# Query projections and expert slots of a PEER layer in one sequence, with the selection of experts in four pieces

## The reference

```python
q = (xc @ w_query).reshape(C, PEER_HEADS, 2, PEER_HALF)          # 8 heads, 2 halves of 128
sc = jnp.einsum('thpd,hpnd->thpn', q, sub_keys)                  # 128 sub-keys a half
top_s, top_i = lax.top_k(sc, 16)
cand_s = (top_s[:, :, 0, :, None] + top_s[:, :, 1, None, :]).reshape(C, PEER_HEADS, 256)
best_s, best_pos = lax.top_k(cand_s, 16)
experts = jnp.take_along_axis(cand_i, best_pos, axis=-1)         # of 16384 experts
gates = jax.nn.softmax(best_s, axis=-1)
u, vv = expert_down[experts], expert_up[experts]
act = jax.nn.gelu(jnp.einsum('cd,chkd->chk', xc, u))
y = jnp.einsum('chk,chkd->cd', gates * act, vv)
```

## Time and profile before

| | us |
|---|---|
| median of three runs (1506.03 to 1508.57) | 1506.32 |
| profiled execution | 1510.51 |
| its span | 1508.7 |
| PE busy | 1271.6 |
| POOL busy | 900.9 |
| DVE busy | 799.8 |
| ACT busy | 598.0 |
| first and last gather issued | 268.1, 918.0 |
| first and last dot starts | 307.9, 939.7 |

### The profile page before, as it was taken

One profiled execution on the slowest core, in us unless ns is written; L12 is line 12 of the kernel. 1 busy time (PEld: TensorE's weight loads), 2 busy tenths in 40 slices (PEclk: granted clock), 3 DMA queues, 4 the chain that ended last, 5 costly groups with the idle time before them and its releaser, 6 DMA issues.

```text
span 1508.7 us, 17575 instructions
## 1 busy us (share of the span) xinstructions
PE 1271.6 (84%) x5876; PEld 903.9 (60%) x5876; DVE 799.8 (53%) x1516; ACT 598.0 (40%) x1247; POOL 900.9 (60%) x541
## 2 busy tenths in 40 slices
PE   6878887868777887777777777899999979799998
PEld 5667767833333333323333333689999968699886
DVE  5943334387776666677777744332453642346401
ACT  5554443343222233332332322346555334455432
POOL 7963575764444435544443441496868954689985
PEclk9998898989999889999888999999999989899999
DMA  7433335899999999999999997364645633346663
GB/s 249 137 125 105 119 126 168 325 375 420 420 420 420 420 420 420 421 420 421 420 413 402 414 421 310 103 198 141 181 127 179 224 102 110 126 156 184 191 188 104
DMA packets 72944, 400.70 MB, mean 266 GB/s; under 512 B 8096, under 2 KB 8352, under 8 KB 39712
## 3 DMA queue, kind: packets, MB, share of 16 engines
q0 software_dynamic: 36864, 268.45, 43.0%
q1 hardware_dynamic: 33696, 123.35, 26.0%
q10 hardware_dynamic: 2304, 7.85, 1.4%
HBM read 396.48 MB, written 3.15 MB: 265 GB/s over the span
## 4 chain that ended last, share of the span: by engine, by line
PE 28%; issue 21%; POOL 19%; DMA 17%; DVE 12%; ACT 2%; POOLq 0%; ACTq 0%; SPq 0%; DVEq 0%
POOL w_lo L1110 16%; DMA arena<-in_experts,arena 15%; PE bank L679 8%; PE bank L502 6%; PE bank L503 6%; PE bank L504 6%; DMA late_rows<-in_experts,arena 2%; DVE arena L1349 1%; DVE arena L1353 1%; DVE arena L1351 1%; POOL stat L1084 1%; POOL arena L1149 1%; DVE arena L1403 1%; DVE arena L1352 1%; ACT arena L967 1%
## 5 line engine op out<-in xcount | busy, mean ns | idle before, releaser
L1110 POOL TENSOR_TENSOR w_lo<-ring,w_hi 128x1024 fp32r<-128x1024 f32 x228 | 574.5, 2538 | 205.3 <-ACT w_hi L829 204.6
L679 PE MATMUL bank<-arena,diag 128*128 128x512 f32 x872 | 431.6, 653 | 123.0 <-ACT diag L973 122.9
L1149 POOL DMA_INDIRECT arena<-in_experts,arena x218 | 245.8, 1127 | 280.5 <-PE bank L679 228.9
L679 PEld LDWEIGHTS bank<-arena,diag 128*128 128x128 f32 x872 | 179.5, 210 | 371.5 <-issue 226.3
L1403 DVE CUSTOM_DVE_ANT_0 arena<-arena 128x1024 f32<-128x1024 f32 x218 | 262.1, 1225 | 157.5 <-DMA arena<-in_experts,arena 157.5
L829 ACT ACTIVATE w_hi<-ring 128x1024 fp32r<-128x1024 f32 x228 | 240.4, 1059 | 239.7 <-PE bank L504 195.7
L502 PE MATMUL bank<-hT_hi,w_hi 128*128 128x256 f32 x864 | 251.8, 291 | 15.4 <-POOL w_lo L1110 7.9
L503 PE MATMUL bank<-hT_lo,w_hi 128*128 128x256 f32 x864 | 249.8, 289 | 0.0
L504 PE MATMUL bank<-hT_hi,w_lo 128*128 128x256 f32 x864 | 249.5, 289 | 0.0
L964 ACT ACTIVATE arena<-arena 128x4 f32<-128x4 f32 x64 | 13.1, 205 | 439.1 <-DVE arena L1403 439.0
L502 PEld LDWEIGHTS bank<-hT_hi,w_hi 128*128 128x128 f32 x864 | 171.6, 199 | 17.2 <-issue 10.4
(11 more groups left out here) (208 smaller groups left out, 1569.9 us busy)
## 6 DMA issues: line engine op xcount, KB each, us to landing
ring<-in_stream SPq DMA_DIRECT2D x228, 512.0 KB, 3.5
arena<-in_experts,arena POOLq DMA_INDIRECT x218, 18.5
kv_park<-arena ACTq DMA_DIRECT2D x8, 256.0 KB, 4.2
arena<-kv_park ACTq DMA_DIRECT2D x1, 2048.0 KB, 8.1
x_res<-in_x SPq DMA_DIRECT2D x2, 512.0 KB, 5.2
arena<-in_mem SPq DMA_DIRECT2D x1, 1024.0 KB, 11.2
arena<-in_sub_keys ACTq DMA_DIRECT2D x1, 1024.0 KB, 5.1
out<-arena SPq DMA_DIRECT2D x2, 512.0 KB, 2.6
```

What stands on the lines that cost most here:

```text
L679: mm = pe.matmul(y_banks[half][:, :], diag[:, slot % DIAGS, :], rows_buf[slot % GATHERS][:, D + 512 * half:D + 512 * half + 512], start=(i ...
L1110: nc.gpsimd.tensor_tensor(w_lo[:, slot, :], ring[:, slot, :], w_hi[:, slot, :].bitcast(F32), ALU.subtract).then_inc(S("lo_made"), 1)
L1149: nc.gpsimd.indirect_dma_start(out=rows_buf[b], out_offset=None, in_=experts, in_offset=bass.IndirectOffsetOnAxis(ap=expert_u[:, slot:slot ...
```

## The change

- The order of queries, sub-scores and slots is one list, `QUERY_ORDER`, that PE and ACT both walk: query 0, sub-scores 0, query 1, then from head 2 on first chunk, sub-scores of the head before, second chunk. Ahead of each of the six chunks of heads 5 to 7 stand four slots, 24 in all. Behind the list slots 24 to 255 follow.
- `queryT` holds two heads instead of eight, so a ninth gather buffer is free from the start. Slots 0 to 35 go round nine buffers; from 36 on all 13 are used.
- POOL makes low parts 0 to 9 first and the others one by one ahead of the gathers that `LO_AT` names.
- The sums of y have banks 4 to 7 and a semaphore of their own, queries and sub-scores take banks 0 to 3 in turn.
- ACT issues the DMAs of the sub-keys and of the gain rows ahead of the sum of squares of ffn, behind a wait for the parked keys and values.
- `select` has four parts: the two halves' top 16, the 256 sums with their top 16, the expert numbers. They stand before dots 5, 8, 11 and 14; those of unit 1 partly before dots 2 and 4 of unit 0. The gates of unit u + 1 are finished before dot 3 of unit u (those of unit 1 before dot 12 of unit 0); ACT forms the exponentials of unit u + 2 behind the fourth group of slots of unit u instead of the third.
- The last four slots are weighted as 2, 1, 1. The scaling of mix's first tile stands ahead of dot 10 of unit 9.

The core of the diff (left out: indexes that only follow the new buffer table, the bank counters, the body of `weigh`, and the lines of `select` that move unchanged):

```diff
+LAST_BATCHES = [(SLOTS - 4, 2), (SLOTS - 2, 1), (SLOTS - 1, 1)]
+PARTS_AT = [5, 8, 11, 14]
+EARLY = 9
+EARLY_USES = 4 * EARLY
 FIRST_LO = 10
-FIRST_GATHERS = 8
+LO_AT = {2: 10, 4: 11, 6: 12, 8: 13, 16: 14, 20: 15, 28: 16, 32: 17, 36: 18, 40: 19}
+BUFFER = [s % EARLY if s < EARLY_USES else (s - EARLY_USES + EARLY) % GATHERS for s in range(SLOTS)]
+USES = [BUFFER[:s + 1].count(BUFFER[s]) for s in range(SLOTS)]
+EARLIER = [max((i for i in range(s) if BUFFER[i] == BUFFER[s]), default=None) for s in range(SLOTS)]
+QUERY_ORDER = [("query", 0, 0), ("query", 0, 1), ("sub", 0), ("query", 1, 0), ("query", 1, 1)]
+for _h in range(2, PEER_H):
+    QUERY_ORDER += [("query", _h, 0), ("sub", _h - 1), ("query", _h, 1)]
+QUERY_ORDER.append(("sub", PEER_H - 1))
+MIXED_FROM = 5
+_order, QUERY_ORDER = QUERY_ORDER, []
+_group = 0
+for _step in _order:
+    if _step[0] == "query" and _step[1] >= MIXED_FROM:
+        QUERY_ORDER.append(("slots", 4 * _group))
+        _group += 1
+    QUERY_ORDER.append(_step)
+MIXED_SLOTS = 4 * _group
...
-        table[key] = (n, chunk, results, last)
+        results += chunk is None and key[0] != "y"
+        if key[0] == "y":
+            bank = 4 + 2 * key[1] + key[2]
+        else:
+            bank = turn % (4 if key[0] in ("query", "sub") else 8)
+            turn = bank + 1
+        table[key] = ((bank, uses[bank]), chunk, results, last)
...
         dot_junk = [A(2048, 1024), A(3072, 1024)]
-        queryT = A(4096, 4096).rearrange("p (h w t) -> p h w t", h=8, w=2)
+        queryT = A(4096, 1024).rearrange("p (h w t) -> p h w t", h=2, w=2)
...
-        rows_buf = [A(16384 + 2048 * i, 2048) for i in range(8)] + [A(4096 + 2048 * i, 2048) for i in range(3)] \
+        rows_buf = [A(16384 + 2048 * i, 2048) for i in range(8)] + [A(6144, 2048), A(4096, 2048), A(8192, 2048)] \
             + [late_rows[:, 2048 * i:2048 * i + 2048] for i in range(2)]
         assert len(rows_buf) == GATHERS
...
-                    sub_scores(h - 1)
-            for t in range(TT):
-                y_banks = [open_bank(pe, ("y", t, half)) for half in range(2)]
-                n_tile = PEER_H * PEER_K
-                for i in range(n_tile):
-                    slot = t * n_tile + i
+            y_banks, q_bank = {}, {}
+            def add_slots(slots):
+                for slot in slots:
+                    t, i = divmod(slot, PEER_H * PEER_K)
+                    if i == 0:
+                        y_banks[t] = [open_bank(pe, ("y", t, half)) for half in range(2)]
+                    last = i == PEER_H * PEER_K - 1
                     pe.wait_ge(S("diag_made"), slot + 1)
                     for half in range(2):
-                        mm = pe.matmul(y_banks[half][:, :], diag[:, slot % DIAGS, :],
-                                       rows_buf[slot % GATHERS][:, D + 512 * half:D + 512 * half + 512],
-                                       start=(i == 0), stop=(i == n_tile - 1))
-                        if i == n_tile - 1:
-                            mm.then_inc(result_done, 1)
-                    if i < n_tile - 1:
+                        mm = pe.matmul(y_banks[t][half][:, :], diag[:, slot % DIAGS, :],
+                                       rows_buf[BUFFER[slot]][:, D + 512 * half:D + 512 * half + 512],
+                                       start=(i == 0), stop=last)
+                        if last:
+                            mm.then_inc(S("y_done"), 1)
+            for step in QUERY_ORDER:
+                if step[0] == "slots":
+                    add_slots(range(step[1], step[1] + BATCH))
+                elif step[0] == "sub":
+                    sub_scores(step[1])
+                else:
+                    _, h, j = step
+                    if j == 0:
+                        q_bank[h] = open_bank(pe, ("query", h))
+                    c = FIRST["query"] + 2 * h + j
+                    wait_weight(c)
+                    transposed_into(q_bank[h][:, j * T:(j + 1) * T], c, normed("ffn") if h == j == 0 else None)
+            add_slots(range(MIXED_SLOTS, SLOTS))
...
-            sumsq("ffn", xs, xn)
-            norm_out("ffn", con("g_ffn"))
             act.wait_ge(S("kv_parked"), 16 * 8)
             act.dma_start(subk, sub_keys).then_inc(S("subk_loaded"), 16)
             act.dma_start(gain_rows, ffn_rows).then_inc(S("gain_loaded"), 16)
-            for h in range(PEER_H + 1):
-                if h < PEER_H:
-                    copy_out(("query", h), queryT[:, h, :, :])
-                if h > 0:
-                    copy_out(("sub", h - 1), scores[:, h - 1, :, :, :])
-            hi_parts(LAST["query"] + RING)
+            sumsq("ffn", xs, xn)
+            norm_out("ffn", con("g_ffn"))
             def gate_exps(u):
...
+            for step in QUERY_ORDER:
+                if step[0] == "slots":
+                    weigh(step[1])
+                    if step[1] == 0:
+                        gate_exps(1)
+                    if step[1] == 3 * BATCH:
+                        gate_exps(2)
+                elif step[0] == "query" and step[2] == 1:
+                    h = step[1]
+                    if h >= 2:
+                        wait_evacuated(act, ("sub", h - 2))
+                    copy_out(("query", h), queryT[:, h % 2, :, :])
+                    if h == 3:
+                        gate_exps(0)
+                elif step[0] == "sub":
+                    copy_out(step, scores[:, step[1], :, :, :])
+            hi_parts(LAST["query"] + RING)
+            for slot in range(MIXED_SLOTS, SLOTS, BATCH):
+                u, b = slot // PEER_K, slot % PEER_K // BATCH
+                if slot < SLOTS - BATCH:
+                    weigh(slot)
+                else:
+                    for i, count in LAST_BATCHES:
+                        weigh(i, count)
+                if b == 3 and u + 2 < UNITS:
+                    gate_exps(u + 2)
+                if u == PEER_H and b == 3:
+                    sumsq("mix", xs, xn, (0,))
...
-                u, b = slot // PEER_K, slot % GATHERS
+                u, b = slot // PEER_K, BUFFER[slot]
                 pool.wait_ge(S("experts_ready"), u + 1)
-                if slot >= GATHERS:
-                    used_by(pool, slot - GATHERS)
-                elif slot >= 8:
+                if EARLIER[slot] is not None:
+                    used_by(pool, EARLIER[slot])
+                elif slot >= EARLY:
                     wait_evacuated(pool, ("sub", PEER_H - 1))
...
-                if slot == FIRST_GATHERS:
-                    lo_parts(LAST["query"] + RING)
+                if slot in LO_AT:
+                    lo_parts(FIRST["query"] + LO_AT[slot])
...
-            def select(u):
+            def select(u, part):
                 t, h = u // PEER_H, u % PEER_H
-                wait_evacuated(dve, ("sub", h))
                 own.sync()
-                for w in range(2):
-                    top16(scores[:, h, t, w, :], top_s[:, w, :], top_u[:, w, :])
...
+                if part < 2:
+                    if part == 0:
+                        wait_evacuated(dve, ("sub", h))
+                    top16(scores[:, h, t, part, :], top_s[:, part, :], top_u[:, part, :])
+                elif part == 2:
+                    own.mark(v.tensor_copy(top_f, top_u))
...
+                    top16(cand, best_s[:, u, :], pos_u)
+                    own.sync()
...
+                else:
+                    own.mark(v.tensor_scalar(half_u[:, 0, :], pos_u, 4, None, ALU.logical_shift_right))
...
-            for u in range(2):
-                select(u)
-            for u in range(2):
-                finish_gates(u)
+            for part in range(4):
+                select(0, part)
+            for part in range(2):
+                select(1, part)
+            finish_gates(0)
             for u in range(UNITS):
                 for k in range(PEER_K):
-                    if k == PEER_K // 2 and u + 2 < UNITS:
-                        select(u + 2)
-                    if k == PEER_K // 2 and u == PEER_H:
+                    if u == 0 and k in (2, 4):
+                        select(1, k // 2 + 1)
+                    if k in PARTS_AT and u + 2 < UNITS:
+                        select(u + 2, PARTS_AT.index(k))
+                    if k == 8 and u == PEER_H:
                         mix_add(0)
+                    if k == 10 and u == PEER_H + 1:
+                        mix_scale(0)
+                    if k == (12 if u == 0 else 3) and u + 1 < UNITS:
+                        finish_gates(u + 1)
                     dot(u * PEER_K + k)
-                if u + 2 < UNITS:
-                    finish_gates(u + 2)
-                if u == PEER_H + 1:
-                    mix_scale(0)
```

More of the change, by code:

```diff
@@ L429, in used_by @@
             if slot % n_tile == n_tile - 1:
[L430 removed]
+                eng.wait_ge(S("y_done"), 2 * (slot // n_tile) + 2)
             else:
@@ L969, in weigh @@
                 own.sync()
-                for i in range(slot, slot + BATCH):
```

(1 more changed line is left out.)

119 lines of the change are left out of this document (52 added, 67 removed).

## The result

| | before | after |
|---|---|---|
| median of five runs, us | 1507.26 | 1514.28 |
| lowest, highest | 1506.03, 1508.76 | 1508.69, 1517.14 |
| profiled execution, its span | 1510.51, 1508.7 | 1508.69, 1506.9 |
| ratio to before, 95% interval | | 1.0048 [1.0025, 1.0070] |

The changed kernel is slower by 3.8 to 10.6 us, though its profiled execution is 1.8 us shorter than that of the kernel before. Of all executions here one, of the kernel before beside the last run, took 1625.34 us at a mean granted clock of 0.735; it is left out of every comparison. The profile resolves this at once, if one asks where the changed part begins. The timeline of PE before has the transposes of the ffn norm's first tile here; ahead of them nothing differs but the two DMAs of sub-keys and gain rows.

What follows compares the result with a forecast made beforehand. The expert stage was taken to wait for gathered rows, at 2.533 us a slot. +0.5 at slot 35 and -4.6 at the tail gave -4.1 us: 1506.4 for the profiled execution, median forecast 1502.2, range 1498 to 1507.

Steps and rivals of the forecast that it cites:

- Sub-keys (a): Ahead of query 0 on PE: sub-keys asked for earlier let it start at 235.0 instead of 239.53, 4.5 us.
- First gather (b, c): Gather start: earlier sub-scores 0 end selection 0 at 257.9, but low part 9 holds the first gather until 261.1.
- Issue to landing of a gather: Early gathers: data moves 2 us after issue, 2.5 us per gather; gather 3, issued at 267.2, lands near 275.5.
- S0: Start of slots 0 to 3 on PE, forecast at 278.5.
- The chain S0 to slots 24: Mixed part on PE and ACT: six groups at 8.6, query chunks, sub-scores and waits of 17.3 sum to 89.9 us.
- Slots 24 to slot 35: Behind the mixed part: slots 24 start at 368.4, gather 33 moves data at 373.3, slots 33 to 35 land by 380.8.
- Pieces and banks: Selection in four pieces, hidden behind transfers, and banks and semaphores of y, adding no instruction: 0 us.
- a sign of being wrong: From the norm of mix on, left unchanged: a move of over 1 us would show the prediction wrong.
- Tail: Last four slots weighted 2, 1, 1: PE ends at 946.8 instead of 951.42, -4.6 us; -2.9 if its clock falls once.
- rival 1: PE's mixed groups: the clock holds through waits of 2.2 and 2.3, sparing three groups 1.7 us each; 1497.1, chance 20%.
- Rival 3: Mixed part: the clock falls twice a cycle, in slots and the next query chunk, 10.2 us more; 1512.4, chance 17%.
- start of the chain +-2: Part of the forecast's range: 2 us either way for when slots 0 start on PE, forecast at 278.5.

Runs made afterwards that it cites:

- the last run: Low parts 11 to 13 moved behind the first four dots, against the rearranged mix with other buffers and first four gathers together: 1488.87 us, ratio 0.9869.
- the ACT-order run: Only ACT's order altered in the mixed part, weights of slot groups made ahead of copies, against the changed kernel: 1498.05 us, ratio to before 0.9928.

## Why the prediction was wrong

The forecast was 1502.2 us in a range of 1498 to 1507, the median is 1514.28. In terms of the sum, the forecast was -4.1 us against the profiled execution; counted from the transposes, that execution of after ended 3.6 us later. The terms below explain this difference of 7.7; the further 3 us or so by which the medians differ more have no trace.

- **Sub-keys (a): right.** 4.5 predicted, 4.4 in the trace of after, 4.4 to 4.7 alone. The transfer cost nothing.
- **First gather (b, c): right in its time, in part by luck.** 26.1 us after the start of query 0 predicted, 26.84 measured (229.74 to 256.58). Low part 9 ended at 256.24 and the selection at 256.28; its last instruction, too, took 1.90 for 0.17 under that low part. The selection ended 26.5 us after the start of query 0 and not 22.9, because three of its instructions were held by low parts; it cost nothing only because low part 9, which the sum rests on, was through in the same moment.
- **Issue to landing of a gather: the step that failed.** I let data move 2 us after the issue and the rows land 2.5 later: 4.5 for gather 0. The DMA view of before had the answer and I did not ask it. The last number of its issue lines is the time from issue to landing (a median where there are several), here for gather 0, issued at 268.06, for gather 1, issued at 269.56, and for gather 3, issued at 272.04:

```profile
arena<-in_experts,arena POOLq DMA_INDIRECT x1, 5.8
...
arena<-in_experts,arena POOLq DMA_INDIRECT x1, 8.1
...
arena<-in_experts,arena POOLq DMA_INDIRECT x1, 10.6
```

  The same view of after, for gather 0, issued at 256.58, and for gather 3, issued at 262.89:

```profile
arena<-in_experts,arena POOLq DMA_INDIRECT x1, 6.9
...
arena<-in_experts,arena POOLq DMA_INDIRECT x1, 11.2
```

  Gather 3, on which S0 hangs, was taken at 8.3 (267.2 to 275.5) and needed 11.2 (262.89 to 274.10). With 1 us of later issues S0 came 47.3 after query 0, not 43.5: 3.8 us.
- **The chain S0 to slots 24: right in its sum, 89.9 predicted, 89.93 measured.** Its waits are 3.64, 2.16, 2.21, 3.58, 2.21 and 3.04 for 3.7, 2.2, 2.3, 3.5, 2.3 and 3.3. Its groups are not all 8.6: two ran in 7.13 behind waits of 2.21 and two took 9.8, but the six add up to 51.31 for 51.6, so that part is luck. This is where the mix lost what it was meant to gain, as the ACT-order run shows.
- **Slots 24 to slot 35: the same term again.** 12.4 us predicted (368.4 to 380.8), 16.6 measured (366.97 to 383.60). Gather 33 was issued 370.74 and dotted 377.58, 6.8 later; the issue was 1 us late and the two slots behind it took 6.0 instead of 5.0. Another 4.2 us. So slot 35 was 8.1 late against query 0, all of it in pieces that contain a gather's landing. Of these 8.1 the landings themselves are 2.9 (gather 3) and some 2 (gather 33), the rest is later issues and the slower pace behind gather 33. No run changed the landing time alone; this is the sum redone with measured terms.
- **The rest of the stage.** Two later chunks cost 3.05 (2.5 predicted); 2.2 came back between slots 47 and 255. Sum at the last landing +7.0 for +0.5.
- **Pieces and banks: right**, 0 for the pieces by the run of their own. The norm of mix after PE's end moved by 0.3. All that follows PE's last slot moved by 1.3, more than the 1 us that the prediction named as a sign of being wrong; but in the second profile of the same kernel it is 1.5 us shorter than in before, so this part varies by more than the sign allows for.
- **Tail: right.** -4.6 predicted, -4.77 in the change, -4.78 alone. The second profile of the change has -3.4: there the last eight slots stood behind a wait of 2.84 and took 15.39 for 14.00, near the -2.9 that the prediction gave for a fall of the clock.
- **The clock.** Against the 8.6 charged for each, rival 1 held for two of six groups (2.9 us won), but two took 9.8 (2.4 lost). Its doubt, the row of 2.27, was one row of several. The trace of before has three groups that took 7.13 behind waits of 2.78 to 2.85, one of them here:

```profile
436.42 7.13 PE L679 MATMUL bank<-arena,diag 128*128 128x512 f32 x16 [2.84 <-ACT diag L973]
```

  Rival 3 did not come: behind the group that ended at 304.00 the chunk was through at 306.86, 2.9 us at the full clock, and the chunks behind the five other groups took as long. As the prediction read the page that it cites (the Trainium skill, TensorE: Matmul & The Clock Gate, "A second HAM failure mode: psum-queue depth-cycling"), all six groups would have been slow; two were not, and behind no wait at all they take 7.03.

The range was too narrow for the same reason: "start of the chain +-2" had no row behind it, and the term occurs twice.

## What to carry to other kernels

Where a step hangs on a transfer, take its time from issue to landing from the DMA view, at the load that it will meet, and count how often the chain passes through such a landing. Interleaving work on two engines needs the in-order engine that serves both (here ACT) to issue each piece when it can run, not in the order of the other engine: against the kernel without a mix the same mix cost 13 us in one order of ACT and nothing in another, and with groups and buffers rearranged as well it gained up to 6 (end of span at 1265.0 for 1271.1). Where an early stage varies from execution to execution, compare two traces from the last place where the code is still the same.

## What the runs showed of the hardware

**DVE and POOL shut each other out.** In the fourteen traces 92 dots overlap a low part between 240 and 440 us. 75 of them end 1.07 to 1.14 us behind it, about the 1.22 that a dot takes alone, and 67 of these took 1.5 to 4.1 us. The other 17 began 0.2 to 0.9 ahead of the low part and took 1.22 or 1.23; there the low part was the longer one, 2.5 to 3.2 for 2.4. Being first in the records (POOL's are rough) does not decide: 13 dots that began up to 0.6 ahead were held all the same. A CAST of 32 columns takes some 0.18 alone and 2.11 to 2.35; MAX8 and FIND_INDEX8 keep their 0.29. Of three low parts in a row DVE waited for all in the run without the mix (one tensor_tensor from 279.01 took 7.76), and in the last run it got a turn behind each. The kernel before shows it too, a CAST of 2.31 at 258.42 beside low parts until 260.68. The Trainium skill (SBUF — State Buffer, section "SBUF: two separate sides") says that the port pair that VectorE and GpSimd share is locked for a whole instruction by whichever starts first, against a VectorE operation in a two-port mode or with two SBUF inputs; the trace agrees: the dot has two inputs in SBUF, either engine can be the one that waits, and the delay moved with POOL in the last run. It is a price of spreading low parts between gathers that the prediction set at nothing.

**The clock behind a wait is not decided by its length alone.** The fourteen traces have 317 groups of 16 matmul records behind a wait for ACT. All 102 behind less than 1.97 us took 7.13. From 1.97 to 2.6 us 31 took 7.13 and 29 took 8.5 or more, from 2.6 to 3.4 us 49 and 65, and behind 3.4 us or more all 41 took 8.5 or more. What decides between 1.97 and 3.4 these runs don't tell.
